# Recurrent heads of a two-layer hybrid block: diagonal tiles moved to ACT, level keys to POOL, diagonal products ahead of the state products

## The chip, the cores and the metric

One core of a Trainium2 chip runs the whole program: TensorE (PE), VectorE (DVE), ScalarE (ACT), GpSimd (POOL) and the DMA queues. The metric is the device time of one execution in microseconds; the number quoted for a kernel is the median of its runs.

## The reference, cut to what matters

The model is two layers over 640 tokens (128 prompt tokens and 512 latent tokens, width 1024). Each layer has a projection into three groups of heads, an output projection, and a mixture of experts. The second group of heads is a gated linear recurrence (HGRN2) in chunks of 64 tokens, run forward and backward over four heads of 64 channels. With `b` the running sum of the log forget gates inside a chunk:

```
o_inter = (q * exp(b)) @ S
a[t,s]  = sum_k q[t,k] * k[s,k] * exp(b[t,k] - b[s,k])      for s <= t
o       = o_inter + a @ v
S       = exp(b_end) * S + (k * exp(b_end - b))^T @ v
```

The change touches only how `a`, the 64 by 64 score tile within a chunk, is put together, and the order of that work.

## The kernel before, in words

The work of the recurrent heads is cut into four **units** per layer, eight in all: two pairs of heads `p`, and for each the forward direction (`d = 0`) and the backward one (`d = 1`). A unit holds two heads on 128 partitions and 640 tokens, as ten 128 by 128 score tiles (two heads, five tiles of tokens) in `aT`.

`exp(b[t] - b[s])` can't be split into a query factor and a key factor for all pairs at once without overflow, so the triangle is cut into six **levels** with halves of m = 32, 16, 8, 4, 2, 1 tokens. At each level the later half of every block of 2m tokens are queries, the earlier half keys, and the reference point `b` lies at the border. The diagonal itself (s = t) has no exponent and is a seventh piece.

One unit goes like this before the change (lines of the kernel before):

- DVE makes the decay exponents of the keys one unit ahead (L1069), ACT takes exp of them, DVE multiplies them into the keys (L1081) and makes the decayed queries (L1084). PE transposes those keys (L1566), DVE copies them out (L1108), PE makes the nine **state products** (L1576, 18 instructions), DVE masks them into `S` (L1115) and runs the eight state steps in order (L1129).
- POOL subtracts the reference for each level, queries and keys apart (L537, L538), ACT takes exp (all of ACT's activations are recorded on L573), and DVE multiplies that into the queries (L1099) and the keys (L1100), 320 columns each. The buffers of `exp`, queries and keys are double.
- POOL multiplies `q` by `k` for the diagonal (L523), after its first two levels. PE sums this over channels with ten small products (L1594), DVE spreads the sums over an identity into `aT` (L1140); this sets all of `aT`.
- For each level PE makes the **scores** (L1601, 20 instructions) into one of two PSUM halves, and DVE copies the level's part into `aT` under a mask (L1150).
- After the scores of the last level but one, PE makes the products of the queries with the states (L1624, "inter"), then the last scores, then the products of `aT` with the values (L1632, "intra").

In forward units PE also makes six products of the adaLN modulation with weights streamed from memory (`row_product`, L1405). ACT copies each result row out, and PE turns it into columns (`ada_columns`, L1412). There is one PSUM row for them, so a product waits until the one before has been copied out. In backward units there are none. After each backward unit the two directions' sum is normalized (ACT, PE, DVE; L1162, L1164), and the next pair of heads begins behind that.

The order on each engine is written out by hand, with semaphores; an engine works strictly through its own list. `g_ps` counts PE's results in PSUM, nine per unit, and `g_used` what DVE has taken out. The next unit's first subtractions on POOL and exponents on ACT run while the unit before ends. At the end of a unit ACT issues two DMAs that store the final states.

Of the kernel before, what the change touches and what calls it, by code (L numbers as in the profile page):

```python
# [13 lines left out]
P = 128  # L14
# [196 lines left out]
def build_program(nc, A, C, outs):  # L211
    y_prompt, y_sample, o_ck, o_cv, o_sf, o_sb = outs
    ctx = ExitStack()
    with ctx:
# [45 lines left out]
        st = sb("st", [P, 3, 8])  # L260
        kout = scr[:, 11, 0:P]
# [59 lines left out]
        lv_d = sem("lv_d"); lv_e = sem("lv_e"); lv_ok = sem("lv_ok")  # L321
# [140 lines left out]
        def _(pool):  # L462
# [26 lines left out]
            for l in range(DEPTH):  # L489
# [16 lines left out]
                for p in range(2):  # L506
                    for d in range(2):
# [6 lines left out]
                        b = pT[:, C_HF + 2 * d + p, :]  # L514
                        for i, m in enumerate(HALVES):
                            if i == 2:

                                if u % 4 == 0:
                                    pool.wait_ge(pt_ps, 2 * NPAIR * (l + 1))
                                    pool.wait_ge(sl_ok, 4 * (l + 1))  # L520
                                if u >= 1:
                                    pool.wait_ge(g_ps, 9 * (u - 1) + 3)
                                nc.gpsimd.tensor_tensor(scr[:, 4, :], pT[:, C_HQ + p, :], decayed[:, 2 * d + p, :],  # L523
                                                        ALU.mult).then_inc(dg_in, 1)
# [6 lines left out]
                            if d == 0:  # L531
                                ref = bv[:, :, m - 1:m].to_broadcast([P, nb, m])
                                q, k = slice(m, 2 * m), slice(0, m)
                            else:
                                ref = bv[:, :, m:m + 1].to_broadcast([P, nb, m])
                                q, k = slice(0, m), slice(m, 2 * m)
                            nc.gpsimd.tensor_tensor(dv[:, :, q], bv[:, :, q], ref, ALU.subtract).then_inc(lv_d, 1)  # L537
                            nc.gpsimd.tensor_tensor(dv[:, :, k], ref, bv[:, :, k], ALU.subtract).then_inc(lv_d, 1)  # L538
# [25 lines left out]
        def _(act):  # L564
# [131 lines left out]
            for l in range(DEPTH):  # L696
# [51 lines left out]
                for p in range(2):  # L748
                    for d in range(2):
# [9 lines left out]
                        for i in range(6):  # L759
# [3 lines left out]
                            if d == 0 and i >= 1:  # L763
                                ada(l, 1, 6 * p + i - 1, ada_row_heads)
                        if d == 0:
                            ada(l, 1, 6 * p + 5, ada_row_heads)
# [113 lines left out]
        def _(dve):  # L880
# [128 lines left out]
            for l in range(DEPTH):  # L1009
# [52 lines left out]
                def decay_keys(p, d):  # L1062
# [4 lines left out]
                    if u >= 1:  # L1067
                        dve.wait_ge(g_ps, 9 * (u - 1) + 1)
# [4 lines left out]
                for p in range(2):  # L1073
                    for d in range(2):
# [11 lines left out]
                        def level(i):  # L1086
# [5 lines left out]
                            if n >= 2:  # L1092
                                dve.wait_ge(g_ps, (n - 2) // 6 * 9 + (n - 2) % 6 + 4)

                            def halves(x, which):
                                return x.rearrange("p (n m) -> p n m", m=2 * m)[:, :, which]
                            qs, ks = (slice(m, 2 * m), slice(0, m)) if d == 0 else (slice(0, m), slice(m, 2 * m))
                            e = scr[:, 2 + i % 2, :]
                            V.tensor_tensor(halves(scr[:, 6 + i % 2, :], qs), halves(q, qs), halves(e, qs), ALU.mult).then_inc(lv_ok, 1)  # L1099
                            V.tensor_tensor(halves(kk[:, i % 2, :], ks), halves(k, ks), halves(e, ks), ALU.mult).then_inc(lv_ok, 1)  # L1100
                        g0 = u * 9
# [3 lines left out]
                        dve.wait_ge(g_ps, g0 + 1)  # L1105
                        if p == 0 and d == 0:
                            dve.wait_ge(cache_out, 16 * 2 * (l + 1))
                        V.tensor_copy(scr[:, 11, :], ps[:, 1536 * ((g0) % 2):1536 * ((g0) % 2) + TOK]).then_inc(g_used, 1)  # L1108

                        dve.wait_ge(g_ps, g0 + 2)  # L1110
                        o = 1536 * ((g0 + 1) % 2)
# [8 lines left out]
                        dve.wait_ge(g_used, g0 + 2)  # L1120
# [707 lines left out]
```

## Time and profile before

| what | value |
|---|---|
| median of 3 runs | 1805.18 us (1804.99 to 1806.71) |
| the profiled execution | 1805.76 us, of which 1803.9 us lie between first and last instruction |
| busy: PE, DVE, ACT, POOL | 88%, 38%, 20%, 18% of the span |
| mean granted TensorE clock | 0.943 of full speed |
| recurrent heads, layer 0 | about 316 to 449 us |
| recurrent heads, layer 1 | about 1199 to 1332 us |

The span is one execution on the chip. Times on a timeline count from its first instruction. A timeline row gives the start, the length, the engine, the line, the operation, what is written and read, how often, and in brackets how long the engine stood idle before it and who released it. Rows that merge several instructions show the stretch from the first start to the last end. The end of one instruction overlaps the start of the next by 0.08 to 0.1 us on DVE and ACT, so a step in a sequence is that much shorter than its row's duration. A row of a stretch gives its bounds and length, the busy time and number of instructions of PE, PEld (the weight loads), DVE, ACT and POOL, then the granted clock, the DMA share and GB/s. A granted clock of 1.00 is 2.4 GHz, and 0.50 is 1.2 GHz.

### The profile page before, as it was taken

How to read it: one execution, taken by the hardware profiler on the slowest of the kernel's cores; microseconds unless marked ns; L12 is line 12 of the kernel's file. 1: busy time of each engine (PE TensorE's matmuls, PEld its weight loads, DVE VectorE, ACT ScalarE, POOL GpSimd, SP SyncE). 2: the span in 40 equal slices, each digit the busy share in tenths (PEclk: the TensorE clock that was granted, in tenths of full speed). 3: DMA queues.
4: the chain of work that ended last, by engine and by line, in shares of the span. 5: the costliest groups of instructions: out<-in, count | busy, mean ns of one | idle time of the engine just before them, and what ended most of it. 6: DMA issues, size and time to landing. Idle time of an engine off the chain costs nothing.

```text
span 1803.9 us, 24901 instructions
## 1 busy us (share of the span) xinstructions
PE 1592.4 (88%) x10358; PEld 1159.0 (64%) x10358; DVE 686.0 (38%) x1230; ACT 369.0 (20%) x694; POOL 316.3 (18%) x305
## 2 busy tenths in 40 slices
PE   6999989777998999999969799988779859999995
PEld 5556567655555788888645556666555458888883
DVE  1284246666115122112156722757641332112224
ACT  2221246221003100000142111642200211000002
POOL 4000159332000000000100001964300010000002
PEclk9999999889998899999979899999879969999997
DMA  9921100422013999999942111013400069999985
GB/s 267 323 52 62 56 27 1 141 69 75 18 52 134 345 367 367 365 366 345 357 164 47 47 48 61 12 36 108 118 2 0 0 244 338 370 360 370 368 305 210
DMA packets 143496, 315.69 MB, mean 175 GB/s; under 512 B 25024, under 2 KB 99192, under 8 KB 130456
## 3 DMA queue, kind: packets, MB, share of 16 engines
q1 hardware_dynamic: 120240, 241.88, 39.5%
q0 software_dynamic: 11104, 37.26, 5.4%
q10 hardware_dynamic: 12040, 34.95, 4.9%
q8 instruction: 83, 1.36, 0.3%
q14 instruction: 29, 0.24, 0.0%
HBM read 279.46 MB, written 34.60 MB: 174 GB/s over the span
## 4 chain that ended last, share of the span: by engine, by line
PE 75%; DVE 11%; ACT 4%; DMA 4%; POOL 3%; issue 3%; ACTq 0%; POOLq 0%; DVEq 0%
PE ps L1764 20%; PE ps L1361 19%; PE ps L1778 10%; PE ps L1405 4%; PE ps L1601 3%; ACT scr L573 3%; PE ps L1481 3%; PE ps L1748 3%; POOL scr L504 2%; DVE scr L974 2%; PE ps L1661 2%; PE ps L1541 1%; PE ps L1504 1%; DMA pT<-h_rows,slot_tok 1%; DMA scr<-y_rows,slot_i 1%
## 5 line engine op out<-in xcount | busy, mean ns | idle before, releaser
L1764 PEld LDWEIGHTS ps<-hT,ring 128*128 128x128 f32 x3200 | 370.2, 194 | 26.6 <-issue 22.0
L1764 PE MATMUL ps<-hT,ring 128*128 128x128 f32 x3200 | 371.1, 277 | 3.4 <-ACT hT L573 3.4
L1361 PE MATMUL ps<-hT,ring 128*128 128x512 f32 x960 | 269.4, 442 | 19.6 <-DVE pT L1020 12.6
L1361 PEld LDWEIGHTS ps<-hT,ring 128*128 128x128 f32 x960 | 149.7, 195 | 141.7 <-issue 128.6
L1778 PE MATMUL ps<-ring,pT 128*128 128x512 f32 x400 | 179.6, 592 | 0.0
L545 POOL DMA_INDIRECT pT<-h_rows,slot_tok x50 | 47.2, 944 | 728.6 <-PE ps L1748 430.2
L573 ACT ACTIVATE pT<-ps 128x256 f32<-128x256 f32 (+3 forms) x74 | 33.4, 457 | 685.2 <-PE ps L1764 495.0
L1316 DVE TENSOR_TENSOR pT<-ps,pT 128x256 f32<-128x256 f32 x50 | 21.3, 425 | 328.5 <-ACT pT L573 328.5
L1361 PE MATMUL ps<-pT,ring 128*128 128x512 f32 (+1 forms) x512 | 139.0, 434 | 1.7 <-ACT pT L573 1.7
L504 POOL TENSOR_SCALAR scr<-scr,st 128x640 f32<-128x640 f32 (+1 forms) x80 | 128.7, 1627 | 43.4 <-DVE st L1029 43.3
L1778 PEld LDWEIGHTS ps<-ring,pT 128*128 128x128 f32 x400 | 72.3, 190 | 72.7 <-issue 72.7
L1361 PEld LDWEIGHTS ps<-pT,ring 128*128 128x128 f32 x512 | 77.4, 191 | 63.3 <-issue 61.2
L1325 DVE COPY pT<-ps 128x1024 f32<-128x1024 f32 x50 | 61.3, 1225 | 135.8 <-PE ps L1778 135.8
L573 ACT ACTIVATE scr<-scr 128x640 f32<-128x640 f32 (+2 forms) x106 | 72.5, 711 | 151.6 <-POOL scr L538 66.8
L1405 PE MATMUL ps<-ring,cond 128*32 128x256 f32 x768 | 97.6, 401 | 2.3 <-DVE pT L1325 1.3
L496 POOL TENSOR_TENSOR scr<-pT,c_cosT 128x512 f32<-128x512 f32 x10 | 12.7, 1266 | 396.6 <-DVE pT L997 396.6
L1601 PE MATMUL ps<-scr,hT 64*128 64x128 f32 x960 | 72.7, 304 | 9.3 <-DVE hT L1100 9.3
L1601 PEld LDWEIGHTS ps<-scr,hT 64*128 64x128 f32 x960 | 65.1, 210 | 19.6 <-DVE hT L1150 10.2
L1180 DVE SCALAR_TENSOR_TENSOR xT<-ps,mods,xT 128x128 f32<-128x128 f32 (+1 forms) x32 | 16.2, 547 | 147.9 <-PE ps L1361 147.9
L573 ACT ACTIVATE scr<-scr,st 128x640 f32<-128x640 f32 (+1 forms) x80 | 58.8, 736 | 46.5 <-DVE st L1041 46.5
L1405 PEld LDWEIGHTS ps<-ring,cond 128*32 128x32 f32 x768 | 43.1, 115 | 38.7 <-issue 8.1
L537 POOL TENSOR_TENSOR scr<-pT 128x320 f32<-128x320 f32 x48 | 39.0, 813 | 157.0 <-DVE hT L1100 157.0
(228 smaller groups left out, 1864.4 us busy)
## 6 DMA issues: line engine op xcount, KB each, us to landing
ring<-in_w_gate_dram SPq DMA_DIRECT2D x50, 1024.0 KB, 7.4
ring<-in_w_up_dram SPq DMA_DIRECT2D x50, 1024.0 KB, 7.7
ring<-in_w_down_dram SPq DMA_DIRECT2D x50, 1024.0 KB, 7.0
ring<-in_w_ada_dram SPq DMA_DIRECT2D x48, 1024.0 KB, 5.7
y_rows<-pT ACTq DMA_DIRECT2D x50, 512.0 KB, 8.1
ring<-in_w_in_dram SPq DMA_DIRECT2D x14, 1024.0 KB, 11.9
h_rows<-scr ACTq DMA_DIRECT2D x10, 512.0 KB, 2.6
ring<-in_w_in_dram SPq DMA_DIRECT2D x16, 256.0 KB, 4.5
```

The lines of the kernel that those rows point to most:

```text
L504: nc.gpsimd.tensor_scalar(probs, probs, st[:, i % 3, 4 * b + 2:4 * b + 3], None, ALU.mult).then_inc(sc_norm, 1)
L537: nc.gpsimd.tensor_tensor(dv[:, :, q], bv[:, :, q], ref, ALU.subtract).then_inc(lv_d, 1)
L545: pool.indirect_dma_start(xg[:, j % XB, :], None, h_dram, bass.IndirectOffsetOnAxis(ap=slot_tok[:, j:j + 1], axis=0)).then_inc(xg_in[j % X ...
L573: return nc.scalar.activation(out, in_, f, **kw)
L1325: V.tensor_copy(yb[:, j, :], ps[:, 2048 + 1024 * j:2048 + 1024 * j + D]).then_inc(dn_sb, 1)
L1361: ins = mm(out[:, a:b], lhs, rhs[:, a:b], start=start, stop=stop, **kw)
L1405: last = mm(row[r, :], cond[:, 2 * k:2 * k + 32], w[:, k, :], start=(k < 2), stop=(k >= KC - 2))
L1481: last = mm(out[:, s * width:(s + 1) * width], hT[:, k, t * P:(t + 1) * P], w[:, k, a:a + width], start=(k == 0), stop=(k == KC - 1))
L1601: return mm(out[:, at:at + P], kk[hs, (i - 1) % 2, t * P:(t + 1) * P], scr[hs, 6 + (i - 1) % 2, t * P:(t + 1) * P], start=True, stop=True)
L1748: last = nc.tensor.transpose(ps[:, k * P:(k + 1) * P], xg[:, i % XB, k * P:(k + 1) * P], ident[:])
L1764: last = mm(bank(2 + j, P, at + c * P), w[:, k, c * P:(c + 1) * P], xk[:, j, k, :], start=(k == 0), stop=(k == KC - 1))
L1778: last = mm(bank(4 + 2 * j + half), hid[:, j, c, :], w[:, c, 512 * half:512 * half + 512], start=(c == 0), stop=(c == 1))
```

## The change

Three things change in each unit, and the counters are renumbered for them.

- **Diagonal.** PE makes the ten diagonal products right behind the transposes, ahead of the state products, into columns of the same PSUM half that lie behind the transposed keys. In forward units the first modulation product comes right behind them, also ahead of the state products. ACT, not DVE, fills `aT`: it copies the ten columns of sums to SBUF, then writes ten 128 by 128 tiles, each the identity scaled per partition by one column. ACT does this between the exponents of levels 1 and 2. The scores of level 0 wait for it.
- **Topmost level.** Level 0 (m = 32) fills whole rectangles of a chunk, so ACT copies them by two plain copies without a mask, behind the exponents of levels 2 and 3. DVE masks only levels 1 to 5.
- **Keys.** POOL multiplies the exponents into the keys. DVE keeps the queries. POOL's list becomes: the diagonal, subtractions of levels 0 and 1, keys 0, subtractions 2, keys 1, and so on. Only in the first unit of a layer does the diagonal stay behind the subtractions of level 1.

The core of the diff, first what POOL runs:

```diff
+                        def diagonal():
...
+                            if u >= 1:
+                                pool.wait_ge(dg_ps, u)
+                            nc.gpsimd.tensor_tensor(scr[:, 4, :], pT[:, C_HQ + p, :], decayed[:, 2 * d + p, :],
+                                                    ALU.mult).then_inc(dg_in, 1)
...
+                        def keys(i):
...
+                            pool.wait_ge(lv_e, n + 1)
+                            if n >= 2:
+                                pool.wait_ge(g_ps, (n - 2) // 6 * 8 + (n - 2) % 6 + 3)
...
+                            nc.gpsimd.tensor_tensor(out, a, e, ALU.mult).then_inc(lvk_ok, 1)
...
+                        if u % 4 != 0:
+                            diagonal()
                         for i, m in enumerate(HALVES):
...
                             if n >= 2:
-                                pool.wait_ge(lv_ok, 2 * (n - 1))
+                                pool.wait_ge(lvq_ok, n - 1)
+                                pool.wait_ge(lvk_ok, n - 1)
...
+                            if u % 4 == 0 and i == 1:
+                                diagonal()
+                            if i >= 1:
+                                keys(i - 1)
+                        keys(5)
```

ACT (`level` is the exponent of a level, `row` the copy of a modulation row, in forward units only):

```diff
-                        for i in range(6):
...
-                            if d == 0 and i >= 1:
-                                ada(l, 1, 6 * p + i - 1, ada_row_heads)
...
+                        level(0)
+                        level(1)
+                        act.wait_ge(dg_ps, u + 1)
+                        if u >= 1:
+                            act.wait_ge(intra_ps, u)
+                        seq(A_(diag, ps[:, 1024:1024 + 2 * TT], ACT.Copy))
+                        for j in range(2 * TT):
+                            ins = A_(aT[:, j, :], ident[:], ACT.Copy, scale=diag[:, j:j + 1])
+                        ins.then_inc(at_init, 1)
+                        row(0)
+                        row(1)
+                        level(2)
+                        level(3)
+                        act.wait_ge(at_init, u + 1)
+                        act.wait_ge(g_ps, 8 * u + 3)
+                        for j in range(2):
+                            k0, q0 = (64 * j, 64 * j + 32) if d == 0 else (64 * j + 32, 64 * j)
+                            A_(aT[k0:k0 + 32, :, q0:q0 + 32],
+                               ps[k0:k0 + 32, 0:1280].rearrange("p (a t) -> p a t", t=P)[:, :, q0:q0 + 32],
+                               ACT.Copy).then_inc(top_used, 1)
+                        row(2)
+                        row(3)
+                        level(4)
+                        row(4)
+                        level(5)
+                        row(5)
```

DVE (`level` is now the multiplication of the queries alone, `masked` the copy under a mask):

```diff
-                            V.tensor_tensor(halves(kk[:, i % 2, :], ks), halves(k, ks), halves(e, ks), ALU.mult).then_inc(lv_ok, 1)
...
-                                V.tensor_tensor(aT, ident[:].unsqueeze(1).to_broadcast([P, 10, P]),
-                                                ps[:, o:o + 10].unsqueeze(2).to_broadcast([P, 10, P]), ALU.mult).then_inc(g_used, 1)
...
+                        state(1)
+                        state(2)
+                        level(2)
+                        for i in range(1, 6):
+                            masked(i)
+                            if i <= 3:
+                                level(i + 2)
                                 state(2 * i + 1)
                                 state(2 * i + 2)
```

PE (`row_product` is one modulation product):

```diff
+                        pe.wait_ge(dg_in, u + 1)
...
+                            last = mm(ps[:, 1024 + a0:1024 + a1 + 1:a1 - a0], scr[:, 4, t * P:(t + 1) * P], blockones[:, 0:P:64],
+                                      start=True, stop=True)
+                        last.then_inc(dg_ps, 1)
+                        if d == 0:
+                            row_product(0)
...
                         if d == 0:
-                            row_product(0)
...
+                            ada_columns(l, 1, 6 * p)
+                            row_product(1)
+
+                        for i in range(6):
                             if i == 0:
...
+                                pe.wait_ge(at_init, u + 1)
+                            elif i == 2:
+                                pe.wait_ge(top_used, 2 * (u + 1))
                             else:
...
+                                pe.wait_ge(g_used, 7 * u + (2 if i == 1 else i))
+                            pe.wait_ge(lvq_ok, u * 6 + i + 1)
+                            pe.wait_ge(lvk_ok, u * 6 + i + 1)
```

## Rows read from the trace of the kernel before

**Rows 1.** The page's chain that ended last, shares of the span by engine

```profile
PE 75%; DVE 11%; ACT 4%; DMA 4%; POOL 3%; issue 3%; ACTq 0%; POOLq 0%; DVEq 0%
```

**Rows 2.** Stretches: the first forward and the first backward unit of layer 1

```profile
1199.30:1233.90 34.60, 29.07 (x291) 21.39 (x291) 20.57 (x35) 9.27 (x17) 10.81 (x13) 0.90 0.57 184
1233.90:1257.60 23.70, 17.60 (x191) 16.38 (x191) 20.81 (x33) 3.39 (x5) 10.27 (x13) 0.86 0.01 3
```

**Rows 3.** Timeline of PE, first forward unit, layer 1 (start us, us, what, idle before)

```profile
1201.82 0.74 PE L1566 MATMUL ps<-c_ident,scr 128*128 128x128 f32 x5 [2.83 <-DVE scr L1081]
...
1205.48 2.47 PE L1576 MATMUL ps<-i_tok,scr 64*128 64x128 f32 x18 [2.93 <-DVE scr L1108]
...
1207.88 3.22 PE L1405 MATMUL ps<-ring,cond 128*32 128x256 f32 x16
...
1211.03 1.28 PE L1594 MATMUL ps<-c_blockones,scr 128*128 128x2 f32 x10
...
1212.77 1.92 PE L1405 MATMUL ps<-ring,cond 128*32 128x256 f32 x16
```

**Rows 4.** Timeline of PE, state products of the other three forward units

```profile
321.95 2.50 PE L1576 MATMUL ps<-i_tok,scr 64*128 64x128 f32 x18 [2.84 <-DVE scr L1108]
...
388.20 2.47 PE L1576 MATMUL ps<-i_tok,scr 64*128 64x128 f32 x18 [2.37 <-DVE scr L1108]
...
1270.64 2.47 PE L1576 MATMUL ps<-i_tok,scr 64*128 64x128 f32 x18 [2.37 <-DVE scr L1108]
```

**Rows 5.** Timeline of PE, the first backward unit of layer 1

```profile
1239.89 1.35 PE L1576 MATMUL ps<-i_tok,scr 64*128 64x128 f32 x18 [2.40 <-DVE scr L1108]
...
1241.17 2.21 PE L1594 MATMUL ps<-c_blockones,scr 128*128 128x2 f32 x10
...
1243.32 5.93 PE L1601 MATMUL ps<-scr,hT 64*128 64x128 f32 x60
...
1252.73 1.39 PE L1601 MATMUL ps<-scr,hT 64*128 64x128 f32 x20 [1.14 <-DVE hT L1100]
...
1256.19 1.39 PE L1601 MATMUL ps<-scr,hT 64*128 64x128 f32 x20
```

**Rows 6.** Timeline of DVE, the same two units

```profile
1203.53 1.07 DVE L1100 TENSOR_TENSOR hT<-decayed,scr 128x320 f32<-128x320 f32 x1
...
1233.86 1.57 DVE L1150 COPY_PREDICATED hT<-c_lvl,ps 128x640 f32<-128x640 uint8 x1 [1.54 <-PE ps L1601]
...
1244.88 0.35 DVE L1129 SCALAR_TENSOR_TENSOR hT<-hT,scr 128x128 f32<-128x128 f32 x1
...
1246.63 0.48 DVE L1099 TENSOR_TENSOR scr<-pT,scr 128x320 f32<-128x320 f32 x1
...
1247.42 1.08 DVE L1129 SCALAR_TENSOR_TENSOR hT<-hT,scr 128x128 f32<-128x128 f32 x2
...
1253.51 0.84 DVE L1150 COPY_PREDICATED hT<-c_lvl,ps 128x640 f32<-128x640 uint8 x1
```

**Rows 7.** Timeline of POOL, the same two units

```profile
1203.29 0.97 POOL L537 TENSOR_TENSOR scr<-pT 128x320 f32<-128x320 f32 x1 [3.99 <-DVE hT L1100]
...
1247.59 0.76 POOL L537 TENSOR_TENSOR scr<-pT 128x320 f32<-128x320 f32 x1 [6.50 <-DVE hT L1100]
...
1256.60 2.12 POOL L523 TENSOR_TENSOR scr<-pT,decayed 128x640 f32<-128x640 f32 x1
```

**Rows 8.** ACT at 62 to 72 us: timeline, then groups by form

```profile
63.91 7.43 ACT L573 ACTIVATE hT<-hT,mods 128x128 f32<-128x128 f32 x16 [2.25 <-DVE hT L929]
L573 ACT ACTIVATE hT<-hT,mods 128x512 f32<-128x512 f32 x8 | 5.7, 706 | 0.0
L573 ACT ACTIVATE hT<-hT,mods 128x128 f32<-128x128 f32 x8 | 3.2, 396 | 2.3 <-DVE hT L929 2.3
```

**Rows 9.** Two stretches of the backward unit, columns as in rows 2

```profile
1242.00:1244.00 2.00, 2.00 (x13) 1.98 (x15) 1.35 (x2) 0.00 (x0) 0.00 (x0) 0.50 0.00 0
1252.00:1254.00 2.00, 1.27 (x20) 1.22 (x20) 1.97 (x5) 0.39 (x1) 1.34 (x2) 1.00 0.00 0
```

More of the change, by code:

```diff
@@ new lines, in masked, with queries @@
+                        def masked(i):
+                            m, n, o = HALVES[i], CH // HALVES[i], 1536 * (i % 2)
+                            qs = slice(m, 2 * m) if d == 0 else slice(0, m)
+                            dve.wait_ge(g_ps, 8 * u + 3 + i)
+                            if i == 1:
+                                dve.wait_ge(top_used, 2 * (u + 1))
+                            def queries(x):
+                                return x.rearrange("p a (n m) -> p a n m", m=2 * m)[:, :, :, qs]
+                            mask = queries(K["lvl"][:, d, i:i + 1, :]).to_broadcast([P, 2 * TT, n, m])
+                            dve.wait_ge(g_used, 7 * u + 1 + i)
+                            V.copy_predicated(queries(aT), mask,
+                                              queries(ps[:, o:o + 1280].rearrange("p (a t) -> p a t", t=P))).then_inc(g_used, 1)
@@ L1578, in _ @@
                         last.then_inc(g_ps, 1)
-                        def row_product(a):
-                            ada_product(l, 1, 6 * p + a, ada_row_heads, (2 * l + 1) * ADA_HALF + 6 * p + a)
                         if d == 0:
-                            row_product(0)
-                        for i in range(7):
-                            g = g0 + 2 + i
-                            out = buffer(g)
+                            ada_columns(l, 1, 6 * p)
+                            row_product(1)
@@ new lines, in _, with scores @@
+                            pe.wait_ge(lvq_ok, u * 6 + i + 1)
+                            pe.wait_ge(lvk_ok, u * 6 + i + 1)
+                            out = ps[:, 1536 * (i % 2):1536 * (i % 2) + 1536]
+                            def scores(h, t):
+                                hs, at = slice(64 * h, 64 * h + 64), HEAD_TILE[h, t] * P
+                                return mm(out[:, at:at + P], kk[hs, i % 2, t * P:(t + 1) * P],
+                                          scr[hs, 6 + i % 2, t * P:(t + 1) * P], start=True, stop=True)
@@ new lines, in _ @@
+                            scores(0, 4).then_inc(lone_ps, 1)
+                            for t in range(4):
+                                scores(1, t)
+                                scores(0, t)
+                            pe.wait_ge(lone_ps, u * 6 + i + 1)
+                            scores(1, 4).then_inc(g_ps, 1)
+                            if d == 0 and i <= 4:
+                                ada_columns(l, 1, 6 * p + i + 1)
+                                if i <= 3:
+                                    row_product(i + 2)
```

125 lines of the change are left out of this document (43 added, 82 removed).

## Prediction

> **What bounds it now.** I began with the chain of waits: PE holds 75% of it over the program [rows 1], but the change touches only the recurrent heads, so I cut that stage by units. In the first forward unit of layer 1 PE works 29.07 of 34.60 us; in the backward unit behind it PE works 17.60 of 23.70 and DVE 20.81 [rows 2]. So two kinds of unit have two limits, and the other six resemble these two.
>
> In a forward unit PE's timeline has one hole of note. The transposes end, PE waits 2.93 us for DVE's copy, and from the state products on it runs without a break to the unit's last scores [rows 3]. The other three forward units wait 2.84, 2.37 and 2.37 us there [rows 4].
>
> In a backward unit there are no modulation products to fill PE. It waits 2.40 us ahead of the state products, and again before each later level's scores (1.14 us at the fifth) [rows 5]. What it waits for is DVE's round per level: mask, query, key, two state steps. Their rows are 0.84, 0.48, 0.48 and 1.08 us [rows 6]; with ends overlapping by 0.08 to 0.1 that is 0.74 + 0.40 + 0.40 + 1.0 = 2.54 us per level, and the scores come at that pace.
>
> **Forward units.** PE's own work is the same; only its order changes. The hole gets the ten diagonal products (1.28 us) and the first modulation product (1.92 at full clock, 3.22 here at half for most of it) [rows 3], together 3.2 to 4.5 us, more than any of the holes. DVE is ready sooner too, because two key products (0.48 and 1.07 us [rows 6]) no longer stand ahead of its copy. So I count the whole hole: 2.93 + 2.84 + 2.37 + 2.37 = 10.5 us.
>
> What could be late next:
> - POOL's diagonal input is made before the unit or in its first steps, and PE reaches it only behind the transposes. It now stands ahead of POOL's first subtractions, which come about 1.6 us later, but POOL does both while the unit before still has its last products and masks to do. Nothing; without that cover 1.6 us per unit.
> - ACT's ten tiles. No row shows a copy scaled by a column, so I bound it. The nearest is an activation with a per-partition bias: 0.396 us for 128 columns, 0.706 for 512; sixteen of them, eight of each, take 7.43 us [rows 8]. That is 0.93 per pair, so each overlaps its neighbour by 0.09, and one tile costs 0.31. Ten cost 2.2 us (7.43 less eight times 0.706, shared by eight, is 0.22 for one) to 4.0. I take 3.1, with 0.4 for the small copy and waits. It runs beside the modulation product, the state products (1.35 to 2.5) and the second modulation product (1.92). Nothing here.
> - ACT's list is now in step with PE: row copies 0 and 1, exponents 2 and 3, two copies of the topmost level (between 0.4 and 0.7 us each by the same rows), row copies 2 and 3. PE needs 3.5 us per level here (1.92 product, 1.3 scores, columns). ACT's share of a level is one exponent of 640 columns (0.8 us by the slope of rows 8), one row copy (0.4 to 0.7) and a part of the two copies: near 2. POOL's two subtractions and one key are 3 x 0.76 = 2.3 us [rows 7]. Both fit.
> - The last two state steps. DVE's query of level 5 now meets the next unit's diagonal on POOL (1.5 to 2.12 us [rows 7]) and the states of "inter" may come up to 0.3 us after PE asks. I charge 0.3 per forward unit, 1.2 in all.
>
> Forward sum: 10.5 - 1.2 = 9.3 us.
>
> **Backward units**, in the times of the unit that begins with the mask at 1233.86 [rows 6]. Transposes end at 1239.89 - 2.40 = 1237.5 [rows 5]. DVE leaves out two keys, 0.48 and 1.07 less the overlap, so its copy is ready 1.4 us sooner, at 1238.5; the diagonal products end at 1238.8. State products run from 1238.8 to 1240.1. The score tiles' start is now ACT's: 1238.8 + 0.1 + 0.3 + 3.1 gives 1242.4, against 1243.32 before: 0.9 us sooner. DVE loses the identity spread and one mask, which don't return elsewhere on it.
>
> Scores 0 and 1 at 1.32 us each end at 1245.0. From there two rounds compete. POOL: key 2 waits for scores 0, then subtraction pairs and keys alternate at 2.3 us per level, so scores 4 could start at 1249.1, against 1252.73. DVE: the mask of level 1 starts at 1245.1, then 0.74 + 0.40 + 1.0 = 2.14 us per level three times, so the eighth state is ready at 1251.5. "Inter" began at 1254.0 before (1252.73 + 1.3) and ends where the last scores begin, at 1256.19 [rows 5]. DVE is the later of the two: 2.5 us sooner without new collisions.
>
> The collisions are the uncertain term. A DVE multiplication of two SBUF operands beside POOL takes 1.07 us instead of 0.48; a pair of state steps takes 1.08 where a lone step takes 0.35; a mask, which reads PSUM, stays at 0.84 beside POOL [rows 6]. POOL's subtraction beside DVE takes 0.97 instead of 0.76 [rows 7]. The new keys on POOL start when scores end, as the mask does, so most of each key falls beside a mask and costs nothing. I charge 0.5 us per backward unit: 2.5 - 0.5 = 2.0. In the backward unit of each layer's first pair POOL runs on into the next unit's diagonal while DVE still has a query and two states to do; one of those waits behind a whole 1.5 us instruction, and a step after it once more, 2.0 us together: gain 0. Two units at 2.0 and two at 0 give 4.0 us.
>
> The Trainium skill, SBUF — State Buffer, section "Who interferes with whom", speaks against this change: a DVE instruction with two SBUF inputs and a GpSimd instruction that reads SBUF exclude each other, and whichever comes first keeps the shared port to its end. The trace agrees in kind [rows 6, 7]; if POOL never paused, the backward units would go as in the second rival.
>
> **Sum.** 9.3 + 4.0 = 13.3 us off the profiled execution's 1805.76: 1792.5. That execution lies 0.6 above the median, so 1792. The expert stages behind the heads run on PE without a break and should only shift.
>
> **The clock** is charged at nothing, with both ends kept. Before, the granted clock is 0.50 at 1242 to 1244 and 1.00 at 1252 to 1254 [rows 9]; the drop followed the 2.40 us hole. At half clock the diagonal took 2.21 instead of 1.28, and three levels' scores 5.93 instead of 3 x 1.32 = 3.96 [rows 5]. In forward units the state products took 2.47 instead of 1.35 [rows 3, 5] and the first product 3.22 instead of 1.92 [rows 3], 2.4 us together. The change closes the hole in forward units and replaces it in backward units by one of about 2.2 us (1240.1 to 1242.4). Best end: no drop, 2.4 more per forward unit and about 1 per backward one. Worst end: third rival.
>
> **Rivals.**
> 1. *POOL and DVE hardly meet, and the clock stays up.* The backward units of the first pairs gain 2.5 like the others: 4 x 2.5 = 10; the clock adds about 1.2 per forward unit: 10.5 + 10 + 4.8 = 25 us, 1780. For it: the masks beside POOL are unslowed. Against: POOL is busy in 10.27 of 23.70 us [rows 2] even without the keys.
> 2. *POOL and DVE take turns through the levels.* Each of the three two-operand steps per level then waits for a whole POOL instruction of 0.7 us: three waits less the 0.35 already in the state pair is 1.75 on top of 2.14 per level, 5.2 over three levels. Against 2.5 gained, each backward unit loses 2.7: 4 x 2.7 = 10.8 against 9.3, that is 1806 to 1807, no change. For it: both engines would have work nearly all the time. Against: masks and POOL's waits for scores break the alternation.
> 3. *Slower: PE sinks to half clock in the backward units and stays there.* Its work now comes in short pieces between waits for ACT and POOL. Price: "inter" takes 2.2 us longer, the last scores 1.32, the products with the values (as many instructions as scores) 1.3, and the first scores 1.3, together 6 us per backward unit. Four units lose 24 against 13.3 gained: 1816. The point from which it decides: backward units longer by over 3.3 us than I forecast. For it: the drop in this very unit before [rows 9]. Against: at 1252 to 1254 PE worked only 1.27 of 2 us and kept its full clock.
> 4. *The change doesn't do what it says:* the state products in forward units wait anyway, because the copy is late behind POOL. Then 9.3 becomes at most 3 and the whole 7: 1798. Against: the copy reads PSUM.
>
> **Numbers.** Forecast (1786 to 1797) 0.55; rival 1 0.20; rival 2 0.10; rival 3 0.08; rival 4 0.07. What a measurement can tell from no change is about 0.2%, 3.6 us, so "same" is 1801.6 to 1808.8. Faster: the forecast, rivals 1 and 4, 0.82. Same: rival 2 with its near side of rival 3, 0.11. Slower 0.07. The range reaches over the forecast, most of rivals 1 and 4, and stops short of rivals 2 and 3: 1778 to 1802.
>
> **What would show it.** Right: in forward units the diagonal products directly behind the transposes, no hole over 0.5 us ahead of the state products, and the unit about 2.3 us shorter. In backward units scores 0 released by ACT about 3.5 us behind the diagonal products; the second pair's unit shorter by 2 us, the first pair's hardly. Wrong: state steps and queries of 0.7 us and more throughout (rival 2); a clock of 0.50 at "inter" (rival 3); the ten tiles over 4 us; a forward unit's scores waiting for ACT's exponents.

## The result and the profile after

The changed kernel takes **1821.62 us** (median of 4 runs, 1819.28 to 1827.73) against 1805.95 for the kernel before in the same session: ratio 1.0081, 95% interval 1.0064 to 1.0097. It is slower by 0.8%, where 0.7% faster was forecast, and lies outside the range. Its profiled execution is the longest of the four (1827.73, span 1825.9, mean granted clock 0.924); the one before had span 1803.9 and clock 0.943.

I cut both profiled executions at the same events of TensorE's timeline: a forward unit from its transposes to its products with the values, a backward unit from there to its own products with the values, and a third stretch from there to the next transposes (or the Fourier products), which holds the norm of the pair.

| us, profiled execution | before | after | difference | forecast |
|---|---|---|---|---|
| four forward units | 133.25 | 123.93 | -9.3 | -9.3 |
| four backward units | 96.12 | 115.93 | +19.8 | -4.0 |
| four stretches behind a pair | 31.41 | 38.21 | +6.8 | 0 |
| everything else | 1543.1 | 1547.8 | +4.7 | 0 |

So the gain came where it was expected, and nearly three times as much was lost behind it. That the sum agrees to a tenth is chance: the four units gained 3.70, 1.05, 2.72 and 1.85 us, where 2.54, 2.07, 2.63 and 2.07 were forecast. The two spans differ by 22.0 us and the medians by 15.7, so about 6 us of the table belong to this one execution. The last line isn't shown to be the change's: in the ten experiments below, which alter nothing there, the same stretches add up to anything from 1539.9 to 1547.3 us.

The first forward unit of layer 1 (timeline of PE; start, duration, instructions, idle before them) answers to [rows 3]:

```profile
1213.10 1.30 PE L1607 MATMUL ps<-c_ident,scr 128*128 128x128 f32 x5 [2.84 <-DVE scr L1128]
1214.19 2.13 PE L1613 MATMUL ps<-c_blockones,scr 128*128 128x2 f32 x10
1216.25 3.37 PE L1448 MATMUL ps<-ring,cond 128*32 128x256 f32 x16
1219.55 1.38 PE L1626 MATMUL ps<-i_tok,scr 64*128 64x128 f32 x18
```

The diagonal products stand right behind the transposes, the first modulation product behind them, and the state products (L1626) follow without a wait: the 2.93 us hole is gone. The transposes, the diagonal and the first product still run at half speed, behind a wait of 2.84 us: the granted clock is 0.50 from 1213 to 1219 us.

The backward unit behind it, with PE's timeline, answers to [rows 5]:

```profile
1244.05 1.31 PE L1677 MATMUL ps<-hT,i_tok 128*64 128x128 f32 x20 [1.70 <-DVE hT L1188]
...
1245.90 1.18 PE L1613 MATMUL ps<-c_blockones,scr 128*128 128x2 f32 x10
...
1250.40 5.36 PE L1647 MATMUL ps<-scr,hT 64*128 64x128 f32 x60 [2.02 <-ACT hT L593]
1256.98 1.39 PE L1647 MATMUL ps<-scr,hT 64*128 64x128 f32 x20 [1.22 <-POOL hT L534]
1259.84 2.23 PE L1647 MATMUL ps<-scr,hT 64*128 64x128 f32 x20 [1.47 <-DVE scr L1144]
1265.00 0.69 PE L1669 MATMUL ps<-scr,hT 128*128 128x64 f32 x2 [2.93 <-DVE hT L1172]
...
1269.03 2.51 PE L1647 MATMUL ps<-scr,hT 64*128 64x128 f32 x20
1273.22 2.40 PE L1677 MATMUL ps<-hT,i_tok 128*64 128x128 f32 x20 [1.68 <-DVE hT L1188]
```

The start of this unit is as forecast: scores 0 are released by ACT 3.3 us behind the diagonal products. What is new is the wait of 2.93 us ahead of the products with the states ("inter", L1669), for DVE's state steps L1172. Before, "inter" followed the fifth scores without a wait in all four units. The fifth scores run at half speed for the most part (2.23 us), and from "inter" on everything takes 1.8 times as long: the last scores 2.51 instead of 1.39 us, the values 2.40 instead of 1.31.

DVE's and POOL's timelines of the same levels, with the masks (L1188), queries (L1144) and pairs of state steps (L1172) on DVE, and the keys (L534) and the next unit's diagonal input (L523) on POOL, answer to [rows 6, 7]:

```profile
1254.35 0.88 DVE L1188 COPY_PREDICATED hT<-c_lvl,ps 128x640 f32<-128x640 uint8 x1 [0.83 <-PE ps L1647]
1255.12 1.00 DVE L1144 TENSOR_TENSOR scr<-pT,scr 128x320 f32<-128x320 f32 x1
1256.04 1.81 DVE L1172 SCALAR_TENSOR_TENSOR hT<-hT,scr 128x128 f32<-128x128 f32 x2
1257.77 0.84 DVE L1188 COPY_PREDICATED hT<-c_lvl,ps 128x640 f32<-128x640 uint8 x1
1258.51 1.23 DVE L1144 TENSOR_TENSOR scr<-pT,scr 128x320 f32<-128x320 f32 x1
1259.66 2.63 DVE L1172 SCALAR_TENSOR_TENSOR hT<-hT,scr 128x128 f32<-128x128 f32 x2
1262.22 0.82 DVE L1188 COPY_PREDICATED hT<-c_lvl,ps 128x640 f32<-128x640 uint8 x1
...
1263.84 1.10 DVE L1172 SCALAR_TENSOR_TENSOR hT<-hT,scr 128x128 f32<-128x128 f32 x2
```
```profile
1255.73 1.11 POOL L534 TENSOR_TENSOR hT<-decayed,scr 128x320 f32<-128x320 f32 x1
...
1258.39 2.21 POOL L534 TENSOR_TENSOR hT<-decayed,scr 128x320 f32<-128x320 f32 x2
1260.57 1.58 POOL L523 TENSOR_TENSOR scr<-pT,decayed 128x640 f32<-128x640 f32 x1
```

From mask to mask DVE needs 3.42 and 4.45 us, and 2.72 more to the eighth state at 1264.94. The queries, 0.48 us before, take 1.00 and 1.23, and a pair of state steps up to 2.63, always beside a POOL instruction. The masks, which read PSUM, keep their 0.82 to 0.88.

The granted clock over the same unit (columns as in [rows 2]) answers to [rows 9]:

```profile
1251.00:1253.00 2.00, 2.00 (x22) 2.00 (x22) 0.00 (x0) 0.60 (x1) 0.00 (x0) 0.50 0.04 8
1257.00:1259.00 2.00, 1.37 (x20) 1.18 (x20) 1.98 (x3) 0.54 (x1) 2.00 (x3) 1.00 0.00 0
1259.00:1261.00 2.00, 1.16 (x13) 1.19 (x15) 1.97 (x3) 0.20 (x1) 2.00 (x3) 0.80 0.00 0
1263.00:1265.00 2.00, 0.00 (x1) 0.00 (x1) 1.97 (x5) 0.00 (x0) 1.57 (x3) 0.50 0.00 0
1277.00:1283.20 6.20, 1.94 (x5) 0.72 (x3) 2.61 (x4) 4.03 (x6) 0.72 (x1) 0.50 0.00 0
```

The clock falls twice. After the wait for ACT's tiles it is at 0.50 (1.2 GHz) and comes back to 1.00 (2.4 GHz). It falls again around 1260, behind the waits of 1.22 us for a key and 1.47 us for a query, before the wait for the states begins, and then stays at half through the rest of the unit and the norm to the next unit's transposes: the +6.8 us of the table's third line. In the second pair of layer 1 it holds a little longer and falls in the 1.75 us wait ahead of "inter" (start 1335.44):

```profile
1332.00:1334.00 2.00, 1.39 (x20) 1.22 (x20) 1.96 (x4) 0.00 (x0) 1.07 (x1) 1.00 0.00 0
1334.00:1336.00 2.00, 0.56 (x3) 0.56 (x3) 1.96 (x5) 0.00 (x0) 0.00 (x0) 0.82 0.00 0
```
```profile
1335.44 0.69 PE L1669 MATMUL ps<-scr,hT 128*128 128x64 f32 x2 [1.75 <-DVE hT L1172]
```

### The profile page after: what moved, and what is told of

Its sections match the earlier page's. It is cut to its first block, busy times and chain, and to the rows that moved or that the text cites. A ratio compares the mean times of both kernels' runs of the same rounds, so it can differ in the third digit from the quotient of the medians.

```text
span 1825.9 us, 25072 instructions
## 1 busy us (share of the span) xinstructions
PE 1618.2 (89%) x10358; PEld 1179.8 (65%) x10358; DVE 667.2 (37%) x1166; ACT 399.2 (22%) x798; POOL 361.4 (20%) x353
## 4 chain that ended last, share of the span: by engine, by line
PE 75%; DVE 10%; ACT 5%; DMA 4%; POOL 3%; issue 2%; ACTq 0%; POOLq 0%; DVEq 0%
PE ps L1809 20%; PE ps L1404 19%; PE ps L1823 9%; PE ps L1448 4%; PE ps L1647 3%; ACT scr L593 3%; PE ps L1524 3%; POOL scr L505 3%; PE ps L1793 3%; DVE scr L1021 2%; ACT hT L593 2%; PE ps L1706 2%; PE ps L1669 1%; PE ps L1584 1%; DVE hT L1188 1%
## 5 line engine op out<-in xcount | busy, mean ns | idle before, releaser
L1404 PE MATMUL ps<-hT,ring 128*128 128x512 f32 x960 | 270.5, 444 | 19.6 <-DVE pT L1067 12.6
L1448 PE MATMUL ps<-ring,cond 128*32 128x256 f32 x768 | 103.2, 418 | 2.0 <-DVE pT L1368 1.3
L1647 PE MATMUL ps<-scr,hT 64*128 64x128 f32 x960 | 79.2, 322 | 17.3 <-ACT hT L593 8.1
L1647 PEld LDWEIGHTS ps<-scr,hT 64*128 64x128 f32 x960 | 70.8, 227 | 28.7 <-issue 19.1
L534 POOL TENSOR_TENSOR hT<-decayed,scr 128x320 f32<-128x320 f32 x48 | 48.5, 1013 | 100.9 <-PE ps L1647 53.9
```

The source lines that it names most:

```text
L534: nc.gpsimd.tensor_tensor(out, a, e, ALU.mult).then_inc(lvk_ok, 1)
L1404: ins = mm(out[:, a:b], lhs, rhs[:, a:b], start=start, stop=stop, **kw)
L1448: last = mm(row[r, :], cond[:, 2 * k:2 * k + 32], w[:, k, :], start=(k < 2), stop=(k >= KC - 2))
L1647: return mm(out[:, at:at + P], kk[hs, i % 2, t * P:(t + 1) * P], scr[hs, 6 + i % 2, t * P:(t + 1) * P], start=True, stop=True)
```

## The experiments

Ten kernels, each an edit of the changed kernel. All ratios are to the kernel before, run in the same session. Differences between two changed kernels are those of their medians. Cuts are marked with "..."; the edits are shortened to what matters.

**Keys back on DVE** (e1_keys_dve).

```diff
-                            if i >= 1:
-                                keys(i - 1)        # POOL
-                        keys(5)
...
+ V.tensor_tensor(out, a, e, ALU.mult).then_inc(lvk_ok, 1)   # DVE, behind the query
```

> The changed kernel with the key multiplications back on DVE (320 columns each, behind the query of the same level); diagonal, ACT tiles and order stay. Theory A (POOL's keys shut DVE's two-operand steps out, the states come late, PE idles, its clock falls): the backward units return to 23 us or less from one unit's products with the values to the next, the granted clock at inter is 1.00, forward units keep their 9 us; about 1790 us. Theory B (the 2.0 us wait for ACT's ten tiles alone brings the clock down): inter still runs at 0.50 and takes 4.1 us; 1805 or more.

Measured: 1812.63 us, ratio 1.0030 (1.0015 to 1.0045), 9.0 us below the changed kernel. "Inter" still waits 1.08 to 2.14 us for the states, and the half clock is still there behind it in the profiled execution:

```profile
1256.82 0.69 PE L1670 MATMUL ps<-scr,hT 128*128 128x64 f32 x2 [1.08 <-DVE hT L1173]
```

So the keys on POOL are a part of the lateness and not all of it. Theory A's 1790 us is missed by 22. The time is theory B's, but its cause isn't shown: in this unit the wait for ACT's tiles is only 0.67 us, and the clock falls in or behind a wait of 2.45 us for a key of DVE. POOL's diagonal input still meets DVE here: a query beside it takes 1.76 us.

**Filler for the clock** (e2_filler). 46 products of the identity into an unused bank in each backward unit, ahead of scores 0, 3, 4 and "inter", so that PE stays busy in its waits.

```diff
...
+ filler((14, 0, 0, 8, 8, 0)[i])    # ahead of scores i, backward units
...
+ filler(16)                        # ahead of "inter"
```

> The changed kernel with idle matmuls (identity times identity into unused columns of a PSUM bank, 46 per backward unit) put where PE waits in backward units: ahead of the scores of levels 0, 3 and 4 and ahead of inter. Nothing else moves. If half clock is the larger part of the loss (theory C), inter, last scores, products with the values and the column sums return to full speed: about 5.5 us per backward unit, 1799 to 1803. If lateness of the states is the larger part (theory A), the clock comes back but the total stays over 1808.

Measured: 1807.98 us, ratio 1.0010 (0.9994 to 1.0025): 13.6 us less, with more work. That lies between theory C's 1799 to 1803 and theory A's "over 1808". The backward units take 27.1 us each with every instruction behind the filler at full speed, and the four stretches behind the pairs 29.2 us instead of 38.2:

```profile
1249.45 3.84 PE L1635 MATMUL ps<-c_ident 128*128 128x128 f32 x32
1253.13 0.33 PE L1677 MATMUL ps<-scr,hT 128*128 128x64 f32 x2
...
1255.18 1.39 PE L1653 MATMUL ps<-scr,hT 64*128 64x128 f32 x20
1258.24 1.31 PE L1685 MATMUL ps<-hT,i_tok 128*64 128x128 f32 x20 [1.68 <-DVE hT L1188]
```
```profile
1249.91 0.71 DVE L1172 SCALAR_TENSOR_TENSOR hT<-hT,scr 128x128 f32<-128x128 f32 x1
```

So the half clock costs the changed kernel at least 13.6 us. Units of 27.1 us at full clock are still 3.1 longer than before, 24.0, but most of that can be the filler's own room: the eighth state is done at 1250.62 (second fence), and the filler holds "inter" back by another 2.5 us. How much lateness costs without the clock can't be read from this run. Nor is all of the 13.6 us new: in the kernel before, the stretches behind the pairs take 31.4 us, 2.2 more than here.

**State steps early** (e3_states_early). In backward units all eight ahead of DVE's query of level 2, where DVE waits for scores 0.

```diff
-                        state(1)
-                        state(2)
+                        early = 8 if d == 1 else 2
+                        for j in range(1, early + 1):
+                            state(j)
                         level(2)
...
+                                if early == 2:
+                                    state(2 * i + 1)
+                                    state(2 * i + 2)
```

> The changed kernel with all eight state steps of backward units ahead of DVE's query of level 2, where DVE idled 2.3 us. Keys stay on POOL. Theory A: inter no longer waits for the states (2.9 and 1.75 us less idle) and the level round loses its two contended steps, so the backward units come back to 24 us or less and the clock holds: 1795 to 1803. Theory B: inter is earlier by 2 us but still at 0.50: 1811 to 1815.

Measured: **1786.58 us** (1785.23 to 1795.07), ratio 0.9908 (0.9882 to 0.9933), 35 us below the changed kernel (31 by the ratios) and faster than before. Theory A's cause held, and the gain is 8 us larger than it said. Backward units take 22.1 us each. DVE does six steps in 2.29 us, in a stretch in which POOL rests:

```profile
1228.40 2.29 DVE L1172 SCALAR_TENSOR_TENSOR hT<-hT,scr 128x128 f32<-128x128 f32 x6
```

PE's timeline of that unit (L1671 is "inter"):

```profile
1228.02 5.36 PE L1649 MATMUL ps<-scr,hT 64*128 64x128 f32 x60 [2.02 <-ACT hT L593]
...
1237.24 1.39 PE L1649 MATMUL ps<-scr,hT 64*128 64x128 f32 x20 [1.25 <-POOL hT L534]
1238.56 0.43 PE L1671 MATMUL ps<-scr,hT 128*128 128x64 f32 x2
```

"Inter" no longer waits, and it has the full clock. The wait of 2.02 us for ACT's tiles is unchanged, and so is the dip to half clock behind it, so that wait and that dip alone are not what the changed kernel lost by.

**POOL's next diagonal held back** until the unit's states are done (e4_pool_gate).

```diff
                         if u % 4 != 0:
+                            pool.wait_ge(s_ok, 8 * u)
                             diagonal()
```

> The changed kernel with one more wait on POOL: the next unit's diagonal and subtractions start only when the unit's eight states are done. If the collision with the next unit's work is what makes the states late (my prediction put 2.0 us on it, in two of four backward units), 4 to 8 us come back: 1814 to 1818. If the keys of the same unit do it, the time stays within 3 us of the changed kernel.

Measured: 1814.21 us, ratio 1.0043 (1.0026 to 1.0059), 7.4 us less. "Inter" waits 1.75 us in all four units, where the first pairs had 2.93 to 2.95. POOL's work for the next unit (the diagonal input and the first subtractions, which the wait holds back together) is worth 1.2 us of lateness in the first pairs; the rest is there without it. The first expectation held.

**State steps behind the masks of before** (e5_states_back: each pair from the second on one mask earlier, keys on POOL).

```diff
                         level(2)
+                        state(3)
+                        state(4)
                         for i in range(1, 6):
                             masked(i)
...
-                                state(2 * i + 1)
-                                state(2 * i + 2)
+                            if i <= 2:
+                                state(2 * i + 3)
+                                state(2 * i + 4)
```

> The changed kernel with each pair of state steps from the second on one level mask earlier, behind the same masks of DVE as in the kernel before (3 and 4 ahead of the mask of level 1, 5 and 6 behind it, 7 and 8 behind the mask of level 2); the keys stay on POOL. If the place behind the mask of level 3 is what makes the last state late, the products with the states in backward units wait for under 0.5 us (2.93 and 1.75 in the changed kernel), the clock stays up in them, and the time falls to 1793 to 1801 us. If the collisions of state steps and queries with POOL's keys are what makes it late, the three pairs still take 1.1 to 2.6 us each, the rounds of DVE stay at 3.4 us and more, the clock still falls, and the time stays above 1808 us.

Measured: 1795.80 us (1794.57 to 1801.84), ratio 0.9929 (0.9910 to 0.9948): the place alone is worth 25.8 us, with what the clock gives back. DVE's and PE's timelines show that the collisions are still there, one mask earlier:

```profile
1235.63 1.81 DVE L1172 SCALAR_TENSOR_TENSOR hT<-hT,scr 128x128 f32<-128x128 f32 x2
...
1239.12 1.06 DVE L1172 SCALAR_TENSOR_TENSOR hT<-hT,scr 128x128 f32<-128x128 f32 x2
...
1242.00 2.63 DVE L1172 SCALAR_TENSOR_TENSOR hT<-hT,scr 128x128 f32<-128x128 f32 x2
```
```profile
1244.68 0.56 PE L1672 MATMUL ps<-scr,hT 128*128 128x64 f32 x2 [1.12 <-DVE hT L1172]
...
1252.77 2.40 PE L1680 MATMUL ps<-hT,i_tok 128*64 128x128 f32 x20 [1.67 <-DVE hT L1188]
```

The pairs take the same 1.81 and 2.63 us as in the changed kernel. The waits at "inter" fall to 1.12 us in the first pairs and none in the second: not under 0.5 everywhere, so the expectation held in its time and only partly in its wait. In the profiled execution, the longest of the four, the half clock stays in both backward units of layer 1 (values at 2.40 us) and in neither of layer 0 (1.31): this version stands near the edge.

**Parts of the change, undone one by one with the state steps early.** The keys, the tiles on ACT and TensorE's order were undone; the topmost level on ACT was not, so what it is worth alone isn't shown. First the keys (e6_early_keys_dve: e3_states_early, and the keys on DVE as in e1_keys_dve).

> The experiment e3_states_early (1786.6 us) with the keys on DVE again. If POOL's keys cost what they save once the state steps are out of their way, the time is 1785 to 1789 us. If the move of the keys is still worth the 0.5 us of DVE's round in each of the three middle levels of four backward units, it is 1790 to 1795 us. If the collisions still cost more than that, it is under 1785 us.

Measured: 1788.03 us, ratio 0.9890 (0.9872 to 0.9909). That can't be told from 1786.58: with the state steps out of the way, moving the keys is worth nothing that shows.

Then the tiles (e7_early_tiles_dve; ACT's copies go):

```diff
...
+ V.tensor_tensor(aT, ident[:].unsqueeze(1).to_broadcast([P, 10, P]),
+     ps[:, 1024:1034].unsqueeze(2).to_broadcast([P, 10, P]), ALU.mult).then_inc(at_init, 1)
```

> The experiment e3_states_early (1786.6 us) with the ten diagonal tiles written by DVE in one operation again, ahead of its state steps (1.49 us in the kernel before, beside ACT's 3.03 us for ten). If the wait of the first scores for ACT's tiles (about 2.0 us in a backward unit) costs time, the wait falls to 1 us or less and the time falls by 3 to 6 us, to 1781 to 1784 us. If the tile operation only pushes the state steps, the mask and the queries back by its own 1.5 us, the time is 1786 to 1792 us.

Measured: 1799.60 us, ratio 0.9953 (0.9938 to 0.9969), a miss beyond both expectations. The edit puts the one operation of 1.48 us behind DVE's masking of the state products, so it ends later than ACT's ten did (7.3 us behind the preceding values instead of 6.3):

```profile
1236.50 5.90 PE L1647 MATMUL ps<-scr,hT 64*128 64x128 f32 x60 [3.04 <-DVE hT L1159]
```

The wait is 3.04 us instead of 2.02. Forward units lose 4.4 us together and backward units 5.1. Against this place on DVE, writing the tiles on ACT is worth 13.0 us (8 by the ratios). All ten tiles in the 1.50 us for which DVE waits ahead of that masking were not tried.

**All units early** (e8_all_early; the edit is to e3_states_early).

```diff
-                        early = 8 if d == 1 else 2
+                        early = 8                  # forward units too
```

> The changed kernel with all eight state steps ahead of DVE's query of level 2 in the forward units too (e3_states_early has them there in backward units alone). In forward units TensorE has the adaLN products to do, so that no wait for the states stands there in the changed kernel: the same 1785 to 1788 us as e3_states_early. If pairs of state steps between the masks delay the masks of forward units beside POOL's keys, the forward units fall from 30.5 to 29.5 us each and the time to 1781 to 1784 us.

Measured: 1787.07 us, ratio 0.9882 (0.9864 to 0.9900): nothing more, as expected. Forward units take 123.5 us together against 121.9.

**Tiles split between ACT and DVE** (e9_early_split).

```diff
-                        for j in range(2 * TT):    # ACT's tiles
+                        for j in range(6):
...
+ V.tensor_tensor(aT[:, 6:10, :], ident[:].unsqueeze(1).to_broadcast([P, 4, P]),
+     diag[:, 6:10].unsqueeze(2).to_broadcast([P, 4, P]), ALU.mult).then_inc(at_init, 1)
```

> The experiment e3_states_early with six of the ten diagonal tiles written by ACT and four by DVE in one operation, in the 1.5 us in which DVE waits for the state products. If the 2.02 us for which the first scores of a backward unit wait for ACT's tiles is still paid, four tiles of 0.30 us fewer on ACT make the wait 0.8 us and each backward unit about 1 us shorter: 4 to 5 us, to 1781 to 1783 us. If what follows (the top copies, the masks, DVE's round) sets the end of the unit anyway, it stays at 1785 to 1788 us. e7_early_tiles_dve, with all ten on DVE, lost 13 us, so a loss is possible too if the operation pushes DVE's multiplication of the state products back: 1788 to 1792 us.

Measured: 1790.59 us (1785.80 to 1801.26), ratio 0.9907 (0.9872 to 0.9942), no gain. The time is the last expectation's, but not for its cause: the multiplication of the state products starts 4.37 us behind the preceding values, as in e3_states_early. The wait for ACT falls from 2.02 to 0.85 us as expected and turns into a wait for DVE's query of level 2, which stands behind the six state steps (2.77 us here, with a key of POOL beside the first of them):

```profile
1234.94 2.50 PE L1653 MATMUL ps<-scr,hT 64*128 64x128 f32 x40 [0.85 <-ACT hT L593]
1240.02 2.07 PE L1653 MATMUL ps<-scr,hT 64*128 64x128 f32 x20 [2.57 <-DVE scr L1145]
```

Where a run is longer its mean clock is lower: 0.953 at 1786.9 us, 0.938 at 1801.3.

**TensorE's order undone**, states early (e10_early_order; the edit in words).

```diff
-                        (diagonal products)        # behind the transposes
-                        row_product(0)
                         (state products)
+                        row_product(0)
+                        (diagonal products)
```

> The experiment e3_states_early with TensorE's order undone: state products, then adaLN row 0, then the diagonal products (in backward units diagonal products right behind the state products). If the order is what fills TensorE's wait for DVE's copy of the transposes, the forward units have a gap of 2 to 3 us again ahead of the state products and the tiles of ACT start 1.4 us and more later: 1.5 to 2 us in each of eight units, 1798 to 1802 us. If the order is worth nothing beside the writing of the tiles by ACT, the time stays at 1785 to 1788 us.

Measured: 1831.52 us, ratio 1.0128 (1.0114 to 1.0143): 45 us above e3_states_early, three times the expectation. PE's timeline of a forward unit:

```profile
1217.25 2.50 PE L1619 MATMUL ps<-i_tok,scr 64*128 64x128 f32 x18 [1.56 <-DVE scr L1151]
...
1223.24 1.28 PE L1628 MATMUL ps<-c_blockones,scr 128*128 128x2 f32 x10
1228.11 1.01 PE L1457 MATMUL ps<-sel,mrow 64*128 64x2 f32 x4 [3.60 <-ACT mrow L593]
```

The hole ahead of the state products is back, 1.56 us. The larger loss is a wait I had not counted: ACT copies modulation row 0 behind its ten tiles, the tiles wait for the diagonal, and PE's next products wait 3.60 us for that row. Forward units lose 32.9 us together and backward units 12.0. So the order is not only a filler: with ACT's list as it is, the tiles need the diagonal products early.

## Why the prediction was wrong

- **Forward units: right in the mechanism, and in the sum partly by luck.** The forecast was 9.3 us and the profile shows 9.3, though unit by unit the gains run from 1.05 to 3.70. POOL's diagonal input, ACT's list and its row copies were covered as the steps said. ACT's ten tiles took 3.03 us (3.1 taken from the bounds 2.2 to 4.0) and the two topmost copies 0.88 together:

```profile
1247.32 3.03 ACT L593 ACTIVATE hT<-c_ident,st 128x128 f32<-128x128 f32 x10
```

- **Backward units, start: right in the first pairs, wrong in the second.** In the first backward unit of layer 1 scores 0 begin 6.35 us behind the values of the unit before, against 7.83 before; 0.9 us was forecast, 1.5 came. In the second they begin 7.92 us behind, against 7.90: this unit starts at half clock, so the values take 2.40 us and the first three scores 6.31. Its mask of level 1 starts 12.6 us behind the values, where 9.6 were forecast. In layer 0 the second pair shows the same 2.40 and 6.31 us, and scores 0 begin 7.91 us behind, against 8.64. Why the clock falls there, ahead of the unit, no run shows.

```profile
1314.85 2.40 PE L1677 MATMUL ps<-hT,i_tok 128*64 128x128 f32 x20 [1.70 <-DVE hT L1188]
...
1322.77 6.31 PE L1647 MATMUL ps<-scr,hT 64*128 64x128 f32 x60 [2.03 <-ACT hT L593]
```
```profile
1327.46 0.87 DVE L1188 COPY_PREDICATED hT<-c_lvl,ps 128x640 f32<-128x640 uint8 x1 [1.57 <-PE ps L1647]
...
1330.23 0.84 DVE L1188 COPY_PREDICATED hT<-c_lvl,ps 128x640 f32<-128x640 uint8 x1
...
1333.52 0.83 DVE L1188 COPY_PREDICATED hT<-c_lvl,ps 128x640 f32<-128x640 uint8 x1
...
1334.65 0.73 DVE L1172 SCALAR_TENSOR_TENSOR hT<-hT,scr 128x128 f32<-128x128 f32 x2
```

- **Backward units, DVE's round: the first term that failed.** The step was "2.14 us per level three times" plus a collision charge of 0.5 us per unit, and 2.0 more in the first pairs. Measured in the first backward unit of layer 1: 3.42 + 4.45 + 2.72 = 10.6 against 6.4 us, so the collisions took 4.2 us instead of 2.5. In the second it is 2.77 + 3.29 + 1.86 = 7.9, so 1.5 us instead of 0.5. In the first unit the mask of level 1 is also 0.7 us later than forecast, and the eighth state comes 20.9 us behind the start of the preceding values; forecast were 16.0 without collisions and 18.5 with their charge, and before it was 18.1. I priced the key on POOL at 0.76 us, the time of a subtraction; it takes 0.86 alone and 1.0 to 1.3 beside DVE. And I argued that the keys would fall beside the masks, which POOL does not slow. In fact, POOL's keys, its subtractions and the next diagonal input reach over the query and the state steps too.
- **The place of the last pair.** The change drops one mask from DVE's loop and lets the pairs of state steps keep their loop number, so the last pair moved from behind the mask of level 2 to behind the mask of level 3. The step counted three rounds but did not ask whether the state steps had to be in the loop that late. e5_states_back shows that the place decides: with the same collisions and the pairs one mask earlier, 25.8 us come back, and with all eight early, 35.
- **The clock charged at nothing: the second failed term, and the larger one.** In the first backward unit of layer 1, 5.4 us beyond the forecast are 0.7 ahead of the mask of level 1, 1.7 in the rounds and 3.0 behind the states: there, at half clock, "inter" takes 4.03 us to the last scores instead of 2.15, and from the last scores to the values it is 4.19 instead of 3.07. In the second, 7.0 us beyond the forecast are 3.0, 1.0 and 3.0 in the same order. The stretches behind the pairs add 6.8 us in all. From the other side, filler takes 13.6 us off the changed kernel (e2_filler). My third rival had this mechanism, with "inter" at half clock, 6 us per unit and a deciding point of 3.3 us beyond the forecast. Its own cause, short pieces between waits, fits the first pairs, where the clock falls ahead of the wait for the states; in the second pairs it falls in that wait. What the rival lacked was its reach: the half clock lasts through the norm behind the unit, which I had not priced.
- **The rivals were taken as alternatives.** I gave the second (turns between POOL and DVE, 1806 to 1807) 0.10 and the third (half clock, 1816) 0.08. Here they come together: DVE's steps are late beside POOL, PE waits for them, and the clock falls in or behind these waits. With the state steps out of the way (e3_states_early) the wait at "inter" and the half clock behind it are gone together, while the dip behind ACT's tiles stays. The time, 1821.6, lies above both prices, and the range, which stopped short of both, could not hold it.

The Trainium skill, SBUF — State Buffer, section "Who interferes with whom", has the rule that the second rival rested on: one of a two-input DVE instruction and a GpSimd instruction reading SBUF keeps the shared port to its end. The trace agrees: six steps take 2.29 us with POOL at rest, and one pair takes 2.63 us beside POOL's second key and diagonal input; masks that read PSUM don't change. And where the two all but start together, the first isn't slowed: a query that starts 0.04 us ahead of a key (1253.03) keeps its 0.49 us, and the key takes 1.17. That the port itself is the reason no run here shows.

Two things stay open: how much of the 13.6 us and of the lateness overlap, since in e2_filler the filler takes room in the same units; and how often the second pairs start at half clock in the changed kernel's other executions, which are 5 to 8 us shorter.

## What to carry to other kernels

When an edit drops one turn of a loop that other work is pinned to by its turn number, write down behind which operation each piece stands before and after; here three pairs of state steps that each slid by one mask were worth 26 us. Put short dependent steps where their engine waits anyway and the engine that slows it rests, and only then weigh which engine should have the rest. In this kernel a late input cost its wait, and beside it what the clock lost in or behind that wait over everything that ran until the clock was back.

## What the runs showed of the hardware

- The clock that fell at about 1260 us stayed at 0.50 through the stretch from 1261 to 1283 us in which PE did inter, scores, values and column sums: waits of 1.2 to 2.9 us were paid for over 22 us. In the first backward unit of layer 1 of e3_states_early, the clock fell to 0.50 behind a wait of 2.02 us, was back at full speed for the fourth scores (1.39 us), and held through waits of 1.23, 1.25 and 1.67 us. Which single wait decides, no run here tells.
- Idle filler work paid for itself: 184 extra products (4 times 46) made the kernel 13.6 us shorter.
- With the other engine at rest, the same multiplication of 128 x 320 by a strided half took DVE 0.48 us and POOL 0.86; POOL's subtraction with a broadcast operand of the same size took 0.72.
